# Paged sample attention reordered: page halves and head pairs outside, four requests inside

## The chip, the core and the metric

The kernel runs on one core of a Trainium2 chip. The metric is the device time of one execution in microseconds (us); lower is better. The median of three runs before the change is 5240.82 us (5238.62 to 5245.79). The profile is of one further execution. Five engines work side by side, each with its own list of instructions: TensorE (PE; its weight loads are listed apart as PEld), VectorE (DVE), ScalarE (ACT), GpSimd (POOL) and SyncE (SP). They meet at semaphores. In this part of the kernel SP and POOL start the transfers from memory.

## The reference

A decoder step of two layers runs over a prompt of 1024 tokens and, with the same weights, over eight sample requests of four new tokens each. A layer mixes three head groups and then applies a gated feed-forward network. The part that matters here is the forgetting attention of the samples: eight heads of 64, and for each request eight cached pages of 128 positions, picked by a page table from a pool.

```python
def fox_sample(q, k, v, logf, k_past, v_past, logf_past):
    c_past = jnp.cumsum(logf_past.astype(F32), axis=1)
    c_new = c_past[:, -1:, :] + jnp.cumsum(logf.astype(F32), axis=1)
    ...
    s_past = jnp.einsum('bthd,bshd->bhts', q, k_past, preferred_element_type=F32) * scale
    s_past = s_past + (cn[..., :, None] - cp[..., None, :])
    s_new = jnp.einsum('bthd,bshd->bhts', q, k, preferred_element_type=F32) * scale
    ...
    p = jax.nn.softmax(jnp.concatenate([s_past, s_new], -1), axis=-1).astype(v.dtype)
    return (jnp.einsum('bhts,bshd->bthd', p[..., :P], v_past)
            + jnp.einsum('bhts,bshd->bthd', p[..., P:], v))
```

Here `k_past = cache_fox_k[l, page_table]`, and `v_past` likewise. All is float32.

## The kernel before

Per layer the order of stages is: projections, RWKV, retention, prompt attention, **sample attention over cached pages**, output projection, feed-forward. TensorE runs them one after the other. The two layers are a hardware loop; inside it the sample attention is a loop `g` over two groups of four requests.

In a group, the 128 rows of a score tile are 4 requests x 8 heads x 4 tokens, so request `b` owns rows 32b to 32b+31 of PSUM. The queries of request `b` and head pair `p` (`cur_q[:, b, p, :]`, 128 x 32) are the stationary operand, so a product for request `b` fills the 32 columns of the array that lead to its 32 rows. Scores are summed over the four head pairs in PSUM banks 0 and 1 (512 cached positions each) and 2 (the four current tokens).

Cached keys arrive with positions on partitions and must be transposed. `key_tr(b, p)` (lines 1269 to 1275) transposes the eight pages of request `b` for head pair `p` into two PSUM banks (3 and 4 for even `p`, 5 and 6 for odd). One copy of 1024 columns brings them to `keyt[p % 2]`: ScalarE for even `p` (line 2152), VectorE for odd (line 1861). Then the products of (b, p) follow, two of 512 columns and one of 4. The loops are request outside, head pair inside, with the transposes one head pair ahead. A float32 product stands in the profile as two records, a float32 transpose as one.

After the last product VectorE takes the maximum (line 1864 on), ScalarE the exponential (line 2154), VectorE normalizes, TensorE transposes the probabilities, and they are copied out (lines 1881, 2157). The value products follow, again request by request: eight pages each, 32 rows of bank 7, 512 columns. VectorE then masks heads (line 1885) and TensorE folds the rows into the output (`F`).

Pages: `slot[b]` holds eight pages of request `b`, first keys, then values in their place. SP loads keys of a request once its last value product of the group before is done (line 508 waits, line 512 issues; for request 3 of a layer's first group it waits for the end of the prompt attention). Values of a request are loaded once its last key transposes are done: five pages by SP (lines 516 and 519), three by POOL (lines 735 to 737). A page number is read from the table in SBUF ahead of each issue. The output weights are loaded after the second group's `F`. In PE's list a helper records every product at line 760 and every transpose at line 764.

Of the kernel before, what the change touches and what calls it, by code (L numbers as in the profile page):

```python
# [21 lines left out]
T = 1024  # L22
DEPTH = 2
DB, TS = 8, 4
# [7 lines left out]
V_SP = 5  # L32
# [82 lines left out]
def build(nc, I, O, decay_rows):  # L115

    ctx = ExitStack()
    with ctx:
# [3 lines left out]
        def sem(name):  # L122
            return ctx.enter_context(nc.semaphore(name))
# [184 lines left out]
        keyt = [region((sil, NP * i), NP) for i in range(2)]  # L308
# [42 lines left out]
        page_in = [sem(f"pages_in{i}") for i in range(4)]  # L351
        vpage_in = [sem(f"last_v_pages_in{i}") for i in range(4)]
# [21 lines left out]
        def job_psum_tm(j):  # L374
# [65 lines left out]
        G_DVE = Steps("cq", "ck", "csel", "creq", *[f"kt{b}{p}" for b in range(4) for p in (1, 3)],  # L440
                      "sn", "mx", "mn", "max", "neg", "sum", "rec", "pn", "pne", "pt1", "pnt", "om", "o")
        G_ACT = Steps(*[f"kt{b}{p}" for b in range(4) for p in (0, 2)], "e", "en", "pt0")
        G_PE = Steps("bias", *[x for b in range(4) for x in [f"T{b}0"] + [y for p in range(4) for y in ([f"T{b}{p + 1}"] if p < 3 else []) + [f"S{b}{p}"]]],
                     "P0", "P1", "Pn", "V0", "V1", "V2", "V3", "F", first=5)
# [6 lines left out]
        def _(sp):  # L451
# [31 lines left out]
            with sp.Fori(0, DEPTH) as l:  # L483
# [14 lines left out]
                with sp.Fori(0, 2) as g:  # L498
                    it = l * 2 + g
                    for b in range(4):  # L500
                        if b == 3:

                            sp.wait_ge(fp_act, FP_ACT.at(l * 2 + 1, "1oT"))
                            sp.wait_ge(lft_out, l * 32 + 32)
                            sp.wait_ge(ko_out, l * 128 + 128)
                            sp.sem_inc(passed, 1)

                        sp.wait_ge(fgr_pe, G_PE.at(it - 1, f"V{b}"))
                        sp.sem_inc(passed, 1)
                        for j in range(NPG):  # L510
                            page = sp.value_load(ptab[0:1, bass.ds(g * (4 * NPG) + (b * NPG + j), 1)], min_val=0, max_val=N_POOL - 1)
                            sp.dma_start(slot[b][:, j, :], I["cache_fox_k"][bass.ds(l, 1), bass.ds(page, 1)].rearrange("a n p h d -> p (a n h d)")).then_inc(page_in[b], 16)

                    for b in range(4):
                        sp.wait_ge(fgr_pe, G_PE.at(it, f"T{b}3"))
                        sp.sem_inc(passed, 1)
                        for j in range(V_SP):
                            page = sp.value_load(ptab[0:1, bass.ds(g * (4 * NPG) + (b * NPG + j), 1)], min_val=0, max_val=N_POOL - 1)
                            sp.dma_start(slot[b][:, j, :], I["cache_fox_v"][bass.ds(l, 1), bass.ds(page, 1)].rearrange("a n p h d -> p (a n h d)")).then_inc(page_in[b], 16)
                    sp.sem_inc(passed, 1)  # L520
# [32 lines left out]
        def _(pool):  # L553
# [18 lines left out]
            with pool.Fori(0, DEPTH) as l:  # L572
# [157 lines left out]
                with pool.Fori(0, 2) as g:  # L730
                    it = l * 2 + g
                    for b in range(4):
                        pool.wait_ge(fgr_pe, G_PE.at(it, f"T{b}3"))
                        pool.sem_inc(passed, 1)
                        for j in range(V_SP, NPG):
                            page = pool.value_load(ptab[0:1, bass.ds(g * (4 * NPG) + (b * NPG + j), 1)], min_val=0, max_val=N_POOL - 1)
                            pool.dma_start(slot[b][:, j, :], I["cache_fox_v"][bass.ds(l, 1), bass.ds(page, 1)].rearrange("a n p h d -> p (a n h d)")).then_inc(vpage_in[b], 16)
# [20 lines left out]
        def _(pe):  # L758
# [68 lines left out]
            with pe.Fori(0, DEPTH) as l:  # L827
# [428 lines left out]
                with pe.Fori(0, 2) as g:  # L1256
                    it = l * 2 + g
                    G_PE.start()
                    gd = lambda n: (fgr_dve, G_DVE.at(it, n))
                    ga = lambda n: (fgr_act, G_ACT.at(it, n))  # L1260
                    ev = lambda b, p: (gd if p % 2 else ga)(f"kt{b}{p}")
# [7 lines left out]
                    def key_tr(b, p):  # L1269

                        if b or p >= 2:
                            pe.wait_ge(*(ev(b, p - 2) if p >= 2 else ev(b - 1, p + 2)))
                        for j in range(NPG):
                            last = tr(ps[:, 3 + 2 * (p % 2) + j // 4, P * (j % 4):P * (j % 4) + P], slot[b][:, j, P * p:P * p + P])
                        G_PE.mark(last, fgr_pe, f"T{b}{p}")

                    for b in range(4):
                        pe.wait_ge(page_in[b], it * ((NPG + V_SP) * 16) + NPG * 16)
                        key_tr(b, 0)
                        for p in range(4):  # L1280
                            if p < 3:
                                key_tr(b, p + 1)
                            pe.wait_ge(*ev(b, p))
                            o = slice(NS * b, NS * b + NS)
                            last_one = p == 3
                            for a in range(2):
                                mm(ps[o, a, :], cur_q[:, b, p, :], keyt[p % 2][:, 512 * a:512 * a + 512], False, last_one)
                            last = mm(ps[o, 2, 0:TS], cur_q[:, b, p, :], cur_k[:, p, TS * b:TS * b + TS], False, last_one)
                            G_PE.mark(last, fgr_pe, f"S{b}{p}")
# [12 lines left out]
                    for b in range(4):  # L1302
                        pe.wait_ge(page_in[b], it * ((NPG + V_SP) * 16) + (NPG + V_SP) * 16)
                        pe.wait_ge(vpage_in[b], it * ((NPG - V_SP) * 16) + (NPG - V_SP) * 16)
                        o = slice(NS * b, NS * b + NS)
                        for j in range(NPG):
                            last = mm(ps[o, 7, :], pts[:, j, o], slot[b][:, j, :], False, j == NPG - 1)
                        G_PE.mark(last, fgr_pe, f"V{b}")
# [52 lines left out]
        def _(v):  # L1361
            def on(*waits):
                for s, val in waits:
                    v.wait_ge(s, val)
# [55 lines left out]
            with v.Fori(0, DEPTH) as l:  # L1420
# [423 lines left out]
                with v.Fori(0, 2) as g:  # L1844
# [11 lines left out]
                    for b in range(4):  # L1856
                        for p in (1, 3):
                            on(gp(f"T{b}{p}"))
                            if b or p == 3:
                                on(gp(f"S{b}1") if p == 3 else gp(f"S{b - 1}3"))  # L1860
                            gm(v.tensor_copy(keyt[1], ps[:, 5:7, :].rearrange("p a b -> p (a b)")), f"kt{b}{p}")
                    on(gp("S33"))
# [21 lines left out]
                    on(gp("V3"))  # L1884
# [36 lines left out]
        def _(a):  # L1921
# [24 lines left out]
            with a.Fori(0, DEPTH) as l:  # L1946
# [193 lines left out]
                with a.Fori(0, 2) as g:  # L2140
# [6 lines left out]
                    for b in range(4):  # L2147
                        for p in (0, 2):
                            on(gp(f"T{b}{p}"))
                            if b or p == 2:  # L2150
                                on(gp(f"S{b}0") if p == 2 else gp(f"S{b - 1}2"))
                            gm(a.copy(keyt[0], ps[:, 3:5, :].rearrange("p a b -> p (a b)")), f"kt{b}{p}")  # L2152
# [124 lines left out]
```

## Time and profile before

| | |
|---|---|
| median of three runs | 5240.82 us |
| span of the profiled execution | 5223.1 us |
| TensorE busy | 4683.3 us, 90% |
| VectorE, ScalarE, GpSimd busy | 1092.1, 654.3, 260.1 us |
| sample attention of layer 0 in the trace | from about 1355 to 1534 us |
| sample attention of layer 1 | from about 3929 to 4108 us |

An engine table gives busy time and its share of the span. The chain of work that ended last is followed back from the last instruction to what released each step. The table of stretches gives busy time, the granted TensorE clock (1.00 is 2.4 GHz, 0.50 is 1.2 GHz) and the DMA rate. In the timeline neighbouring instructions of one kind are merged, with their count behind an x; the square bracket has the idle time ahead of them and what ended it.

### The profile page before, as it was taken

Reading aid. Unit: us, or ns where it says so; the run is one execution under the profiler, and the core shown is the slowest. Engines: PE = TensorE matmul, PEld = TensorE weight load, DVE = VectorE, ACT = ScalarE, POOL = GpSimd, SP = SyncE. Lnnn points to the kernel's source line nnn. Section 1 sums busy time; section 2 is a strip of 40 time slices with the busy share of each in tenths; the row PEclk is TensorE's granted clock in tenths of the full one; section 3 lists DMA queues with packets and bytes.
Section 4 is the critical chain, followed back from the end, with each engine's and each line's share of the span. In section 5 each row is a group of like instructions: output and inputs, shape, how many; then the busy total and the mean of one; then the engine's idle time right before and its main releaser. Section 6 shows DMA issues by size and latency. Waiting matters only on the chain.

```text
span 5223.1 us, 55407 instructions
## 1 busy us (share of the span) xinstructions
PE 4683.3 (90%) x20862; PEld 3164.5 (61%) x20862; DVE 1092.1 (21%) x2491; ACT 654.3 (13%) x1105; POOL 260.1 (5%) x456
## 2 busy tenths in 40 slices
PE   7688888988889999999995879898888999999998
PEld 4477576755445666666654766666653456666665
DVE  2344222133212000000024541312332110000001
ACT  0222011133100000000003220102231000000000
POOL 1000002100000000000010000130000000000000
PEclk8888787989899999999997888798998999999999
DMA  3300101102241111111112001011024211112011
GB/s 75 17 0 0 38 21 23 42 26 65 93 139 33 36 40 36 36 41 34 39 38 5 0 5 41 13 35 42 13 65 157 86 33 36 36 36 58 22 34 61
DMA packets 274079, 215.20 MB, mean 41 GB/s; under 512 B 23696, under 2 KB 236912, under 8 KB 272640
## 3 DMA queue, kind: packets, MB, share of 16 engines
q1 hardware_dynamic: 255296, 163.64, 12.2%
q0 software_dynamic: 18624, 49.50, 3.4%
q8 instruction: 93, 1.52, 0.1%
q14 instruction: 66, 0.54, 0.1%
HBM read 197.55 MB, written 15.53 MB: 41 GB/s over the span
## 4 chain that ended last, share of the span: by engine, by line
PE 82%; DVE 7%; issue 5%; ACT 3%; DMA 3%; DVEq 0%; POOL 0%; ACTq 0%; POOLq 0%; SPq 0%
PE ps L760 79%; PE ps L764 3%; DMA out_rwkv_shift_sample<-big 1%; DVE hT L1379 1%; ACT wd L2136 1%; DMA big<-in_x_prompt 0%; DVE big L1571 0%; DMA wd<-in_state_rwkv 0%; ACT wd L2123 0%; ACT big L2106 0%; DMA out_y_prompt<-big 0%; ACT sil L2152 0%; DVE sil L1372 0%; DVE big L1579 0%; DVE big L1541 0%
## 5 line engine op out<-in xcount | busy, mean ns | idle before, releaser
L760 PE MATMUL ps<-hT,ring 128*128 128x352 f32 x6528 | 1966.1, 463 | 25.6 <-DVE hT L1379 10.7
L760 PEld LDWEIGHTS ps<-hT,ring 128*128 128x128 f32 x6528 | 1246.7, 192 | 738.7 <-issue 29.1
L760 PE MATMUL ps<-big,wd 128*128 128x352 f32 (+3 forms) x2576 | 711.6, 439 | 65.5 <-ACT big L1969 42.3
L760 PEld LDWEIGHTS ps<-big,wd 128*128 128x128 f32 (+2 forms) x2576 | 462.5, 192 | 311.5 <-ACT big L1969 42.6
L1901 DVE TENSOR_TENSOR big<-ps,sil 128x1056 f32 x44 | 55.3, 1258 | 1189.5 <-PE ps L760 1189.5
L760 PE MATMUL ps<-wd 128*128 128x128 f32 (+4 forms) x1560 | 235.0, 297 | 70.0 <-ACT wd L2136 21.7
L760 PE MATMUL ps<-big 128*128 128x128 f32 (+4 forms) x1488 | 244.0, 337 | 52.5 <-POOL big L636 14.8
L760 PEld LDWEIGHTS ps<-wd 128*128 128x128 f32 (+2 forms) x1560 | 207.1, 203 | 136.5 <-issue 76.2
L760 PE MATMUL ps<-ring,hT 128*128 128x128 f32 (+1 forms) x2304 | 261.5, 275 | 0.0
L764 PE MATMUL ps<-ident,big 128*128 128x128 f32 (+4 forms) x998 | 175.4, 322 | 95.4 <-ACT big L1992 28.3
L760 PEld LDWEIGHTS ps<-ring,hT 128*128 128x128 f32 (+1 forms) x2304 | 256.9, 183 | 5.2 <-issue 2.4
L760 PEld LDWEIGHTS ps<-big 128*128 128x128 f32 (+2 forms) x1488 | 203.5, 222 | 86.1 <-issue 16.7
L764 PEld LDWEIGHTS ps<-ident,big 128*128 128x128 f32 (+4 forms) x998 | 131.3, 162 | 123.3 <-issue 67.5
L2164 ACT ACTIVATE sil<-ps 128x1056 f32<-128x1056 f32 x44 | 46.3, 1051 | 1162.8 <-PE ps L760 1162.8
L760 PE MATMUL ps<-sil,wd 128*128 128x64 f32 (+2 forms) x544 | 175.4, 438 | 3.6 <-ACT sil L2152 3.6
L1906 DVE TENSOR_TENSOR xT<-ps,xT 128x1056 f32<-128x1056 f32 x16 | 20.1, 1257 | 599.9 <-PE ps L760 599.9
L2123 ACT ACTIVATE wd<-wd,big 128x256 f32<-128x256 f32 (+7 forms) x128 | 99.2, 775 | 301.7 <-DVE big L1805 301.7
L764 PE MATMUL ps<-ident,wd 128*128 128x128 f32 (+1 forms) x644 | 104.2, 298 | 35.7 <-DVE wd L1877 18.1
L760 PE MATMUL ps<-big,sil 64*128 64x64 f32 (+4 forms) x560 | 116.9, 391 | 8.3 <-DVE sil L1710 8.3
L760 PE MATMUL ps<-ring,wd 128*128 128x128 f32 (+1 forms) x584 | 90.2, 300 | 36.5 <-ACT wd L2136 25.7
L760 PE MATMUL ps<-big,ring 128*128 128x352 f32 x384 | 121.4, 459 | 0.0
L760 PE MATMUL ps<-sil 64*128 64x256 f32 (+4 forms) x608 | 81.8, 420 | 40.6 <-DVE sil L1489 37.7
(336 smaller groups left out, 3122.6 us busy)
## 6 DMA issues: line engine op xcount, KB each, us to landing
big<-in_cache_fox_k SPq DMA_DIRECT2D x128, 256.0 KB, 2.9
ring<-in_w_in SPq DMA_DIRECT2D x60, 512.0 KB, 3.8
ring<-in_w_gate SPq DMA_DIRECT2D x44, 512.0 KB, 3.8
ring<-in_w_up SPq DMA_DIRECT2D x44, 512.0 KB, 3.8
wd<-in_w_down SPq DMA_DIRECT2D x16, 1408.0 KB, 7.0
big<-in_cache_fox_v SPq DMA_DIRECT2D x80, 256.0 KB, 4.0
big<-in_cache_fox_v POOLq DMA_DIRECT2D x48, 256.0 KB, 4.3
ring<-in_w_out SPq DMA_DIRECT2D x16, 512.0 KB, 4.1
```

The source lines that it names most:

```text
L760: return pe.matmul(out, lhsT, rhs, start=start, stop=stop, skip_group_check=True)
L764: return pe.transpose(out, in_, ident[0:n, 0:n])
L1379: NRM_DVE.mark(v.scalar_tensor_tensor(hT[:, k, :].rearrange("p (a b) -> p a b", a=3), xT[:, k, :].rearrange("p (a b) -> p a b", a=3), col( ...
L1901: v.tensor_tensor(big[:, bass.ds((q * 2 + u) * NT, NT)].rearrange("p (a b) -> p a b", a=3), job_psum(1), sil[:, u * NT:(u + 1) * NT].rearr ...
L1906: v.tensor_tensor(xk, job_psum(j), xk, ALU.add).then_inc(evac[j % 2], 1)
L2123: fm(act(sp_[:, s % 2, 0:w], sp_[:, s % 2, 0:w], ACT.Exp, bias=nmx[:, s:s + 1], accum_out=rsum[:, s:s + 1]), f"{u}e{s}")
L2136: fm(a.copy(ptt[:, 0, 0:s // 2 + 1, :], ps[:, 4:6, :].rearrange("p a (b c) -> p (a b) c", c=P)[:, 0:s // 2 + 1, :]), f"{u}pt{s}")
L2164: act(sil[:, u * NT:(u + 1) * NT].rearrange("p (a b) -> p a b", a=3), job_psum(0), ACT.Silu).then_inc(evac[0], 1)
```

## The change

Scores are computed by steps `s = 0..7`, `s = 4a + p`: a page half `a` (four pages, HP = 4) and a head pair `p`, with all four requests inside. A step transposes four pages of each request into one bank per request (3 to 6); four copies of 512 columns, ScalarE for requests 0 and 2, VectorE for 1 and 3, bring them to `keyt[s % 2][:, b, :]`; four products of 512 columns follow, one per request, and in the first page half the four small ones. The transposes of step s+1 are listed ahead of the products of step s. `keyt[1]` moves from `sil` to `ring`. The value products go page by page with the four requests inside, half by half. Page loads go by halves: values of half `a` after the last transposes of that half, keys of the second group's half `a` after the value products of that half. Of each half SP loads two pages per request and POOL two (POOL takes no part in the keys of the first group). The loop over the groups is written out on SP, POOL and TensorE.

```diff
-        keyt = [region((sil, NP * i), NP) for i in range(2)]
+        HP = NPG // 2
+        keyt = [region((sil, 0), 4, HP * PG), region((ringf, 0), 4, HP * PG)]
...
-                with sp.Fori(0, 2) as g:
-                    it = l * 2 + g
-                    for b in range(4):
...
-                        sp.wait_ge(fgr_pe, G_PE.at(it - 1, f"V{b}"))
...
-                    for b in range(4):
-                        sp.wait_ge(fgr_pe, G_PE.at(it, f"T{b}3"))
-                        for j in range(V_SP):
...
+                for g in range(2):
+                    if g:
+                        for a in range(2):
+                            sp.wait_ge(fgr_pe, G_PE.at(l * 2, f"V{a}"))
+                            sp.sem_inc(passed, 1)
+                            for j in (HP * a, HP * a + 1):
+                                for b in range(4):
+                                    key_page(1, b, j)
+                    for a in range(2):
+                        sp.wait_ge(fgr_pe, G_PE.at(l * 2 + g, f"T{4 * a + 3}3"))
+                        sp.sem_inc(passed, 1)
+                        for j in (HP * a, HP * a + 1):
+                            for b in range(4):
+                                value_page(g, b, j)
...
+                    for a in range(2):
+                        pool.wait_ge(fgr_pe, G_PE.at(l * 2 + g, f"T{4 * a + 3}3"))
+                        for j in (HP * a + 2, HP * a + 3):
+                            for b in range(4):
...
-                with pe.Fori(0, 2) as g:
+                for g in range(2):
...
-                    for b in range(4):
-                        pe.wait_ge(page_in[b], it * ((NPG + V_SP) * 16) + NPG * 16)
-                        key_tr(b, 0)
-                        for p in range(4):
-                            if p < 3:
-                                key_tr(b, p + 1)
-                            pe.wait_ge(*ev(b, p))
-                            o = slice(NS * b, NS * b + NS)
-                            last_one = p == 3
-                            for a in range(2):
-                                mm(ps[o, a, :], cur_q[:, b, p, :], keyt[p % 2][:, 512 * a:512 * a + 512], False, last_one)
+                    def key_tr(s):
+                        a, p = s // 4, s % 4
+                        if p == 0:
+                            pe.wait_ge(kpage_in[a], l * (6 * HP * 16) + g * (2 * HP * 16) + 4 * HP * 16)
+                            if g:
+                                pe.wait_ge(kpage_more[a], l * (2 * HP * 16) + 2 * HP * 16)
+                        for b in range(4):
+                            if s:
+                                pe.wait_ge(*ev(s - 1, b))
+                            for j in range(HP):
+                                last = tr(ps[:, 3 + b, P * j:P * j + P], slot[b][:, HP * a + j, P * p:P * p + P])
+                            G_PE.mark(last, fgr_pe, f"T{s}{b}")
+                    def key_scores(s):
+                        a, p = s // 4, s % 4
+                        pe.wait_ge(*ev(s, 2))
+                        pe.wait_ge(*ev(s, 3))
+                        for b in range(4):
+                            last = mm(ps[o4[b], a, :], cur_q[:, b, p, :], keyt[s % 2][:, b, :], False, p == 3)
+                        if a == 0:
+                            for b in range(4):
+                                last = mm(ps[o4[b], 2, 0:TS], cur_q[:, b, p, :], cur_k[:, p, TS * b:TS * b + TS], False, p == 3)
+                        G_PE.mark(last, fgr_pe, f"S{s}")
+                    for s in KS:
+                        key_tr(s)
+                        if s:
+                            key_scores(s - 1)
+                    key_scores(7)
...
-                    for b in range(4):
...
-                        for j in range(NPG):
-                            last = mm(ps[o, 7, :], pts[:, j, o], slot[b][:, j, :], False, j == NPG - 1)
+                    for a in range(2):
+                        pe.wait_ge(vpage_in[a], it * (2 * HP * 16) + 2 * HP * 16)
+                        pe.wait_ge(vpage_more[a], it * (2 * HP * 16) + 2 * HP * 16)
+                        for j in range(HP * a, HP * a + HP):
+                            for b in range(4):
+                                last = mm(ps[o4[b], 7, :], pts[:, j, o4[b]], slot[b][:, j, :], False, j == NPG - 1)
+                        G_PE.mark(last, fgr_pe, f"V{a}")
...
+                    for s in KS:
+                        for b in (1, 3):
+                            on(gp(f"T{s}{b}"))
+                            if s >= 2:
+                                on(gp(f"S{s - 2}"))
+                            gm(v.tensor_copy(keyt[s % 2][:, b, :], ps[:, 3 + b, :]), f"kt{s}{b}")
...
+                    for s in KS:
+                        for b in (0, 2):
+                            on(gp(f"T{s}{b}"))
+                            if s >= 2:
+                                on(gp(f"S{s - 2}"))
+                            gm(a.copy(keyt[s % 2][:, b, :], ps[:, 3 + b, :]), f"kt{s}{b}")
```

## Rows read from the trace of the kernel before

**Rows 1.** Page: busy us, share and instructions of engines; chain by engine.

```profile
PE 4683.3 (90%) x20862; PEld 3164.5 (61%) x20862; DVE 1092.1 (21%) x2491; ACT 654.3 (13%) x1105; POOL 260.1 (5%) x456
...
PE 82%; DVE 7%; issue 5%; ACT 3%; DMA 3%; DVEq 0%; POOL 0%; ACTq 0%; POOLq 0%; SPq 0%
```

**Rows 2.** Stretches, layer 0: length, busy PE, PEld, DVE, ACT, POOL, clock, DMA share, GB/s.

```profile
1359.00:1364.80 5.80, 5.80 (x20) 3.90 (x21) 1.22 (x1) 1.01 (x1) 0.00 (x0) 0.50 0.00 0
...
1373.00:1408.40 35.40, 34.46 (x171) 17.14 (x169) 7.35 (x6) 6.08 (x6) 5.25 (x10) 1.00 0.55 184
...
1417.90:1422.80 4.90, 4.90 (x7) 1.06 (x7) 0.00 (x0) 0.00 (x0) 0.00 (x0) 0.50 0.00 0
```

**Rows 3.** Timeline of TensorE, score stretch: start, us, engine, line, operation, count.

```profile
1359.12 3.67 PE L764 MATMUL ps<-ident,big 128*128 128x128 f32 x16
...
1366.62 1.90 PE L760 MATMUL ps<-sil,wd 128*32 128x512 f32 x4
...
1368.49 0.86 PEld L764 LDWEIGHTS ps<-ident,big 128*128 128x128 f32 x8
...
1369.51 1.90 PE L760 MATMUL ps<-sil,wd 128*32 128x512 f32 x4
```

**Rows 4.** Timeline of TensorE, value products of group 0, near a request change.

```profile
1417.90 25.01 PE L760 MATMUL ps<-big,hT 128*32 128x512 f32 x64
...
1425.49 0.14 PEld L760 LDWEIGHTS ps<-big,hT 128*32 128x32 f32 x3 [0.32 <-issue]
1425.92 0.14 PEld L760 LDWEIGHTS ps<-big,hT 128*32 128x32 f32 x2 [0.29 <-issue]
1426.35 0.14 PEld L760 LDWEIGHTS ps<-big,hT 128*32 128x32 f32 x2 [0.29 <-issue]
```

**Rows 5.** Timeline of TensorE, norm sums in three column groups of 32, output projection.

```profile
1568.97 0.79 PE L760 MATMUL ps<-sil,ones 128*32 128x352 f32 x6
1569.69 2.63 PE L760 MATMUL ps<-hT,ring 128*128 128x352 f32 x8
```

**Rows 6.** Timeline, where the stages of both groups begin and end.

```profile
1408.40 0.16 DVE L1864 TENSOR_TENSOR hT<-ps,wd 128x4 f32<-128x4 f32 x1 [2.34 <-PE ps L760]
...
1442.95 0.69 DVE L1885 TENSOR_TENSOR wd<-ps,wd 128x512 f32<-128x512 f32 x1 [27.17 <-PE ps L760]
...
1449.58 3.67 PE L764 MATMUL ps<-ident,big 128*128 128x128 f32 x16
...
1498.02 0.16 DVE L1864 TENSOR_TENSOR hT<-ps,wd 128x4 f32<-128x4 f32 x1 [2.34 <-PE ps L760]
...
1507.52 24.58 PE L760 MATMUL ps<-big,hT 128*32 128x512 f32 x64
...
1532.13 0.69 DVE L1885 TENSOR_TENSOR wd<-ps,wd 128x512 f32<-128x512 f32 x1 [26.74 <-PE ps L760]
```

**Rows 7.** Timeline, copies of 512 PSUM columns on ScalarE and VectorE.

```profile
1414.05 0.59 ACT L2157 COPY hT<-ps 128x512 f32<-128x512 f32 x1 [2.38 <-PE ps L764]
...
1414.90 0.69 DVE L1881 COPY hT<-ps 128x512 f32<-128x512 f32 x1 [1.83 <-PE ps L764]
```

**Rows 8.** Timeline of page issues by SP, POOL; page: KB, us to landing.

```profile
1370.45 5.05 SPq L519 DMA_DIRECT2D big<-in_cache_fox_v  x5
...
1385.43 0.54 POOL L737 DMA_DIRECT2D big<-in_cache_fox_v  x1 [0.79 <-issue]
...
big<-in_cache_fox_v POOLq DMA_DIRECT2D x48, 256.0 KB, 4.3
```

**Rows 9.** Stretches as in rows 2: keys by SP alone, both queues.

```profile
1346.00:1356.00 10.00, 2.70 (x9) 1.74 (x10) 5.06 (x11) 0.00 (x0) 0.00 (x0) 0.50 0.71 215
...
1475.00:1480.00 5.00, 4.70 (x29) 2.79 (x28) 1.23 (x1) 1.18 (x2) 0.54 (x1) 1.00 1.00 355
```

**Rows 10.** Stretches as in rows 2, near the end: transposes alone, with pauses.

```profile
5193.00:5201.40 8.40, 4.82 (x39) 3.58 (x34) 2.90 (x5) 3.17 (x4) 1.60 (x3) 1.00 0.32 127
5201.50:5213.00 11.50, 8.34 (x36) 6.54 (x35) 2.38 (x4) 4.84 (x5) 2.13 (x4) 0.50 0.52 208
```

More of the change, by code:

```diff
@@ L31 @@
 N_POOL = DB * NPG * 5 // 4
-V_SP = 5
 EPS = 1e-6
@@ L350, in build @@
         decay_out, past_in = sem("decay_rows_out"), sem("past_gates_in")
-        page_in = [sem(f"pages_in{i}") for i in range(4)]
-        vpage_in = [sem(f"last_v_pages_in{i}") for i in range(4)]
+        kpage_in = [sem(f"k_pages_in{i}") for i in range(2)]
+        vpage_in = [sem(f"v_pages_in{i}") for i in range(2)]
+        kpage_more = [sem(f"k_pages_in_pool{i}") for i in range(2)]
+        vpage_more = [sem(f"v_pages_in_pool{i}") for i in range(2)]
         table_in, lft_out = sem("table_in"), sem("log_gates_out")
@@ L439, in build @@
         FS_DVE = Steps("qz", *[f"q{p}{k}" for p in range(4) for k in range(2)], "lfs", "lfn", "ncs")
-        G_DVE = Steps("cq", "ck", "csel", "creq", *[f"kt{b}{p}" for b in range(4) for p in (1, 3)],
+        KS = range(8)
+        G_DVE = Steps("cq", "ck", "csel", "creq", *[f"kt{s}{b}" for s in KS for b in (1, 3)],
                       "sn", "mx", "mn", "max", "neg", "sum", "rec", "pn", "pne", "pt1", "pnt", "om", "o")
-        G_ACT = Steps(*[f"kt{b}{p}" for b in range(4) for p in (0, 2)], "e", "en", "pt0")
-        G_PE = Steps("bias", *[x for b in range(4) for x in [f"T{b}0"] + [y for p in range(4) for y in ([f"T{b}{p + 1}"] if p < 3 else []) + [f"S{b}{p}"]]],
-                     "P0", "P1", "Pn", "V0", "V1", "V2", "V3", "F", first=5)
+        G_ACT = Steps(*[f"kt{s}{b}" for s in KS for b in (0, 2)], "e", "en", "pt0")
+        G_PE = Steps("bias", *[x for s in KS for x in [f"T{s}{b}" for b in range(4)] + ([f"S{s - 1}"] if s else [])], "S7",
+                     "P0", "P1", "Pn", "V0", "V1", "F", first=5)
         block = ctx.enter_context(nc.Block())
@@ L1255, in _ @@
                 last.then_inc(fs_pe, 1)
-                with pe.Fori(0, 2) as g:
+                for g in range(2):
                     it = l * 2 + g
@@ new lines, in _ @@
+                    o4 = [slice(NS * b, NS * b + NS) for b in range(4)]
+                    def key_tr(s):
+                        a, p = s // 4, s % 4
+                        if p == 0:
+                            pe.wait_ge(kpage_in[a], l * (6 * HP * 16) + g * (2 * HP * 16) + 4 * HP * 16)
+                            if g:
+                                pe.wait_ge(kpage_more[a], l * (2 * HP * 16) + 2 * HP * 16)
[5 more added lines that the diff above has]
+                            G_PE.mark(last, fgr_pe, f"T{s}{b}")
@@ new lines, in key_scores @@
+                    def key_scores(s):
[5 more added lines that the diff above has]
+                        if a == 0:
+                            for b in range(4):
+                                last = mm(ps[o4[b], 2, 0:TS], cur_q[:, b, p, :], cur_k[:, p, TS * b:TS * b + TS], False, p == 3)
+                        G_PE.mark(last, fgr_pe, f"S{s}")
@@ L1301, in _ @@
                     mm(ps[:, 7, :], pnt[0:NS, :], vn[0:NS, :], True, False)
[L1302 to L1306, printed above, removed]
-                            last = mm(ps[o, 7, :], pts[:, j, o], slot[b][:, j, :], False, j == NPG - 1)
-                        G_PE.mark(last, fgr_pe, f"V{b}")
+                    for a in range(2):
+                        pe.wait_ge(vpage_in[a], it * (2 * HP * 16) + 2 * HP * 16)
+                        pe.wait_ge(vpage_more[a], it * (2 * HP * 16) + 2 * HP * 16)
+                        for j in range(HP * a, HP * a + HP):
+                            for b in range(4):
+                                last = mm(ps[o4[b], 7, :], pts[:, j, o4[b]], slot[b][:, j, :], False, j == NPG - 1)
+                        G_PE.mark(last, fgr_pe, f"V{a}")
                     pe.wait_ge(*gd("om"))
@@ L1855, in _ @@
                     gm(v.tensor_copy(cur_req, sreq[:, bass.ds(g, 1), :].rearrange("p a b -> p (a b)")), "creq")
[L1856 to L1862, printed above, removed]
+                    for s in KS:
[4 more added lines that the diff above has]
+                            gm(v.tensor_copy(keyt[s % 2][:, b, :], ps[:, 3 + b, :]), f"kt{s}{b}")
+                    on(gp("S7"))
                     past = ps[:, 0:2, :].rearrange("p a b -> p (a b)")
```

53 lines of the change are left out of this document (21 added, 32 removed).

## Prediction

> **What bounds the kernel now.** First the engine table and the chain of work that ended last: TensorE is busy for 90% of the span and carries 82% of the chain, DMA 3% [rows 1]. A change pays if it shortens what TensorE does or waits for. Next the busy time by stretch over the stage that is edited, the cached-page attention of layer 0. In the score stretch (1373.0 to 1408.4) TensorE is busy for 34.5 of 35.4 us at the full granted clock, VectorE for 7.4, ScalarE for 6.1 [rows 2]. TensorE is the bound there too, and pages come in time. The clock is 0.50 (1.2 GHz) for the first 5.8 us of that stage and for the first 4.9 us of the value products, each after a wait [rows 2].
>
> Then the timeline, for what TensorE does with its time. One round of a request and head pair starts with four half-products (a float32 product is recorded as two) of 32 x 512 at 1366.62; eight transposes follow at 1368.49; the next round's products start at 1369.51 [rows 3]. So a round takes 2.89 us: 1.87 for products (four at 0.43, 0.15 for the small current-token ones and the switch), 1.02 for transposes (0.86 for eight weight loads, the rest switch). Each product has 32 stationary columns, a quarter of the array's width, and in this order all products of one request go to the same quarter, so they queue. The value products are 64 such records, one request after the other: 25.01 us [rows 4].
>
> What happens when two requests meet: within a request a weight load starts every 0.43 us; at the change of request, near 1425.5, 3, 2 and 2 start in three successive 0.43 us [rows 4]. The last records of one request and the first of the next run side by side, at undiminished pace. And where three column groups are addressed in turn, in the norm sums, six records of 352 columns are through in 0.72 us (1568.97 to the next work at 1569.69) [rows 5]; at 0.30 us each, from the weights products' pace scaled by width (0.43 x 352 / 512), six in a line would be 1.78. Three quarters thus run together.
>
> **The change part by part.** The order of requests and head pairs is turned inside out. Four requests now stand inside, each in its own quarter.
>
> Scores: 16 rounds per group of four requests become 8, of a head pair and a page half. A new round has 16 transposes (1.02 + 0.86 = 1.88) and 8 half-products of 512 columns in four quarters, two slots deep: 2 x 0.43 + 0.15 = 1.01. That is 2.89 us, the price of an old round, for twice the work. Eight are 23.1. The clock's low start stays: 5.7 us of it at half speed cost 2.85 more, so 26.1. Before: 1408.40 - 1359.12 = 49.3 in the first group, 1498.02 - 1449.58 = 48.4 in the second [rows 3, 6]. Saved 23.2 and 22.3. Old rounds also lost about 1 us per request at its start; that goes with them.
>
> Evacuation: 32 copies of 1024 columns become 64 of 512 over both groups of a layer and both engines. A round has two on ScalarE (0.59 each) and two on VectorE (0.69) [rows 7], 1.4 us at most, beside 2.89 us of TensorE. The transposes of round s+1 into a bank wait for its copy of round s, which has the 1.01 us of products as its cover; the last copy, some 0.2 after its transposes plus 0.69, just fits. I cost it at nothing; without the cover it is 0.7 per round, 22 us in all, an upper bound. The added waits at the head of each product group hold back only those products and the transposes behind them, on TensorE, by the same amount.
>
> Values: 64 records in four quarters are 16 slots, 6.9 us, plus 2.45 for 4.9 us of low clock and 0.13 of lead: 9.5. Before: 1442.95 - 1417.90 = 25.05 and 1532.13 - 1507.52 = 24.6 [rows 4, 6]. Saved 15.5 and 15.1.
>
> The unknown is whether four quarters of 512 columns run as freely as two of 512 and three of 352 do. Bounds: all four free, or pairs only (priced below); I take four, since the row of three is nearest and shows no loss beyond 0.13 us a burst. The Trainium skill, "TensorE: Matmul & The Clock Gate", Part 3 on packing small matmuls, measured 2.38 times for three column tiles; the burst here makes 1.78 / 0.72 = 2.5. Carried to a continuous stream as 0.79 of the ideal, its figure would put 1.8 us on the values and 1.8 on the scores of each group, so some 14 in all, near 5113; the undiminished pace at the change of request [rows 4] speaks for the larger gain.
>
> Loads: a page is 256 KB, a half of four requests 16 pages or 4.19 MB, eight by SP and eight by POOL. SP issues one per 1.18 us ((5.05 - 0.35) / 4), POOL one per 0.54 + 0.79 = 1.33, and POOL's land 4.3 later [rows 8]. With 1 us from release to first issue POOL's eighth lands after 1 + 7 x 1.33 + 4.3 = 14.6. Together the queues ask for over 400 GB/s; the most that a 5 us stretch here moved is 355 [rows 9], by which a half needs 11.8 us plus start and landing. I take 15. Upper bound: the 215 GB/s that SP alone reached [rows 9], 19.5 plus 4.5, so 24.
>
> Where that lies: (a) first-group keys are all issued before the stage, nothing changes. (b) Value half 0 is released in the middle of the scores, 23 us ahead of its use. (c) Value half 1 is released by the last transposes; from there to its use are 2.1 of products, 9.7 of softmax as before and about 5.9 of value half 0: 17.7 against 15, hidden with 2.7 to spare. (d) Second-group keys, half 0, are released when value half 0 is consumed; TensorE then has 3.4 of value half 1 and the 6.6 between 1442.95 and 1449.58 [rows 6], so 10.1, and waits 4.9 for the rest. Before, pages of the first request went out a quarter into the value products and this cost nothing; it is the one new wait. Behind it on TensorE stands the whole second group. (e) Its half 1 queues behind half 0 and lands about 26 to 28 after the release, needed at 15 + 4 x 2.89 + 2 = 28.6: just hidden. On SP nothing but the output weights stands behind, and those wait for the group's end in either kernel; POOL has only later outputs.
>
> Sum for a layer: 23.2 + 15.5 + 22.3 + 15.1 - 4.9 = 71.2, for both 142.4. The profiled span of 5223.1 becomes 5080.7. The runs' median lies 17.7 above that span, so **5098 us**, 2.7% less. This kernel's runs can tell about 0.2% from no change; that is my bound of "same".
>
> **The rivals.**
> Pairs only: two quarters at a time, as the change of request shows for 512 columns [rows 4]. Rounds of 3.75 and values of 16.3: per layer 16.4 + 8.7 + 14.0 + 8.3 = 47.4, time 5146. Against: three in [rows 5].
> Loads become the bound: two queues add no bandwidth, a half takes 24. Then (d) waits 13.9, (e) about 6, (c) 15 and 11: 41 more per layer, time 5180; at 280 GB/s only 13 more in all, 5111. For: a whole half is asked for at once. Against: 355 GB/s with both queues at work [rows 9].
> The clock: in the new rounds TensorE spends more time on transposes (1.72) than on products (0.86). If the clock were 1.2 GHz throughout the scores, a round would be 5.8 and a stage 46: 20 more per stage, 5179. For 8.4 us near the end transposes alone, with pauses, ran at granted 1.00 [rows 10], though at 0.50 after that. The same page of the Trainium skill, Part 4 on transposes, says that they do not count as busy for the clock in the same way, which is this rival; the stretches of [rows 10] bear it out only in the second one.
> Slower: the quarters take turns, because the array changes quarter with each record. Place: scores and values. Eight slots in a round make 5.5 us, a stage 47, saving 2 at best; the values lose the overlap that they have now at three changes of request: 27.5 + 2.6 = 30.1, 5 more. Net some 3 per group, 5253 us, and more if each change of quarter exposed its weight load. It decides once the overlap is under 1.05-fold. [rows 5] is against it.
> Better than forecast: keys arrive in time and the small products vanish under the others: 12 less, 5086.
>
> **How the numbers follow.** Forecast 0.67, loads 0.11 (mostly at the mild end), pairs 0.08, better 0.06, clock 0.04, slower 0.04. The range 5078 to 5152 takes in forecast, better, pairs and mild loads. Faster 0.94, within 0.2% 0.02, slower 0.04.
>
> **What would show it.** In the profile after: the 64 value records of a group in about 9.5 us, four weight loads per 0.43; eight rounds of 2.9; first transposes of the second group waiting about 5 us for cached keys; no wait for pages before value half 1. It is wrong if records of different quarters start 0.43 apart, if clock 0.50 lies in the rounds, or if DMA ends waits elsewhere.

## The result, and the profile after

The changed kernel takes 5091.14 us in the median (5090.70 to 5091.69), the kernel before, run beside it on the same chip, 5241.09. The ratio is 0.9722 with a 95% interval from 0.9703 to 0.9742: 2.8% faster. 5098 was forecast.

The timeline of TensorE in the first group's scores of layer 0, with VectorE's first step of the softmax at its end. It answers to rows 3 and 6.

```profile
1362.75 6.20 PE L783 MATMUL ps<-ident,big 128*128 128x128 f32 x32
1368.88 1.06 PE L779 MATMUL ps<-sil,wd 128*32 128x512 f32 x8
...
1369.91 1.97 PE L783 MATMUL ps<-ident,big 128*128 128x128 f32 x16
1371.81 1.07 PE L779 MATMUL ps<-ring,wd 128*32 128x512 f32 x8
...
1380.60 1.07 PE L779 MATMUL ps<-sil,wd 128*32 128x512 f32 x8
1381.59 1.97 PE L783 MATMUL ps<-ident,big 128*128 128x128 f32 x16
1383.49 1.06 PE L779 MATMUL ps<-ring,wd 128*32 128x512 f32 x8
...
1388.38 0.16 DVE L1895 TENSOR_TENSOR hT<-ps,wd 128x4 f32<-128x4 f32 x1 [1.19 <-PE ps L779]
```

Eight half-products of 512 columns, four quarters two deep, are through in 1.03 us with the small ones (1368.88 to 1369.91), where four in one quarter took 1.87 with theirs [rows 3]. A round is 2.93 us with the small products (1368.88 to 1371.81) and 2.89 without (1380.60 to 1383.49). No row between them shows idle time: the copies are hidden. The scores last from 1362.75 to 1388.38, 25.6 us, where they took 49.3 [rows 3, 6].

The value products of that group: TensorE's row, its weight loads, and VectorE's head mask that ends them.

```profile
1397.87 9.11 PE L779 MATMUL ps<-big,hT 128*32 128x512 f32 x64
...
1401.29 0.20 PEld L779 LDWEIGHTS ps<-big,hT 128*32 128x32 f32 x4 [0.66 <-issue]
1402.09 0.12 PEld L779 LDWEIGHTS ps<-big,hT 128*32 128x32 f32 x4 [0.60 <-issue]
1402.52 0.12 PEld L779 LDWEIGHTS ps<-big,hT 128*32 128x32 f32 x4 [0.31 <-issue]
...
1407.06 0.69 DVE L1916 TENSOR_TENSOR wd<-ps,wd 128x512 f32<-128x512 f32 x1 [11.31 <-PE ps L779]
```

Four weight loads start per 0.43 us, where there was one (and 3, 2, 2 at a change of request) [rows 4]: all four quarters stream at once, none slowed by the others. 9.2 us from 1397.87 to 1407.06, against 25.05.

What is new is a wait. The start of the second group on TensorE, the DMA row of the page for the keys that POOL now loads (KB, us to landing), and the stretch of the wait with the columns of rows 2:

```profile
1410.26 2.10 PE L779 MATMUL ps<-wd 64*128 64x512 f32 x6 [1.39 <-DVE wd L1886]
1419.82 4.99 PE L783 MATMUL ps<-ident,big 128*128 128x128 f32 x32 [7.46 <-DMA big<-in_cache_fox_k]
...
big<-in_cache_fox_k POOLq DMA_DIRECT2D x32, 256.0 KB, 5.7
...
1407.10:1419.80 12.70, 3.16 (x14) 2.03 (x15) 1.61 (x6) 0.00 (x0) 5.37 (x10) 0.70 1.01 353
```

TensorE stands idle for 7.46 us until cached keys are there, while the DMA engines are busy throughout at 353 GB/s, about the 355 of [rows 9] and for more than twice as long.

The stage of a layer is measured below from the start of VectorE's last small copy ahead of the first group (line 1855 before, 1886 after) to the start of the head mask of the second. "Rest" is the profiled span without both stages. Medians are of each kernel's own runs.

| kernel | stage, layer 0 | layer 1 | rest | median |
|---|---|---|---|---|
| before, first profile | 177.2 | 177.0 | 4868.9 | 5241.1 |
| before, profiled again | 176.1 | 174.2 | 4882.7 | 5226.8 |
| changed kernel | 104.1 | 106.2 | 4879.9 | 5091.1 |
| changed kernel, again | 104.2 | 104.3 | 4882.2 | 5098.4 |
| values by request | 117.8 | 119.0 | 4888.8 | 5118.2 |
| scores in one quarter | 144.6 | 144.8 | 4877.8 | 5173.6 |
| loads on SP alone | 140.6 | 140.2 | 4874.1 | 5160.1 |
| before with values interleaved | 151.3 | 151.4 | 4877.0 | 5199.1 |
| keys released by page | 100.5 | 100.4 | 4886.1 | 5088.5 |
| no second keys | 97.3 | 97.0 | 4876.6 | 5072.4 |
| by page, idle-time products | 100.1 | 99.0 | 4879.9 | 5080.8 |

The stage repeats within 3 us; the rest, which no kernel edits, varies by 20 over these eleven executions and by 14 between the two of the kernel before. So mechanisms are read from the stage, and medians confirm what is larger than about 10 us.

### The profile page after: what moved, and what is told of

It is laid out like the page before. It is cut to its first block, busy times and chain, and to the rows that moved or that the text cites. A ratio compares the mean times of both kernels' runs of the same rounds, so it can differ in the third digit from the quotient of the medians.

```text
span 5090.1 us, 55376 instructions
## 1 busy us (share of the span) xinstructions
PE 4538.9 (89%) x20862; PEld 3131.7 (62%) x20862; DVE 1097.4 (22%) x2523; ACT 659.4 (13%) x1137; POOL 287.2 (6%) x504
## 4 chain that ended last, share of the span: by engine, by line
PE 81%; DVE 7%; issue 5%; DMA 3%; ACT 3%; DVEq 0%; POOL 0%; POOLq 0%; SPq 0%; ACTq 0%
PE ps L779 77%; PE ps L783 4%; DMA out_rwkv_shift_sample<-big 1%; DVE hT L1410 1%; ACT wd L2167 1%; DMA big<-in_x_prompt 0%; DVE big L1602 0%; DMA wd<-in_state_rwkv 0%; ACT big L2137 0%; ACT wd L2154 0%; DVE sil L1403 0%; DVE big L1610 0%; DMA out_y_prompt<-big 0%; DMA big<-in_cache_fox_k 0%; DVE big L1574 0%
## 5 line engine op out<-in xcount | busy, mean ns | idle before, releaser
L783 PE MATMUL ps<-ident,big 128*128 128x128 f32 (+4 forms) x998 | 171.9, 322 | 109.7 <-ACT big L2023 26.8
L783 PEld LDWEIGHTS ps<-ident,big 128*128 128x128 f32 (+4 forms) x998 | 133.5, 164 | 144.6 <-issue 66.2
L779 PE MATMUL ps<-ring,wd 128*128 128x128 f32 (+1 forms) x712 | 107.1, 354 | 36.5 <-ACT wd L2167 25.7
L783 PE MATMUL ps<-ident,wd 128*128 128x128 f32 (+1 forms) x644 | 104.3, 298 | 36.1 <-DVE wd L1908 18.2
L783 PEld LDWEIGHTS ps<-ident,wd 128*128 128x128 f32 (+1 forms) x644 | 83.4, 158 | 42.7 <-DVE wd L1908 21.9
```

Source lines behind the costliest of these rows:

```text
L779: return pe.matmul(out, lhsT, rhs, start=start, stop=stop, skip_group_check=True)
```

## Experiments

**The kernel before, profiled again.** No edit. Question: why did its first profile lie 18 us under the median?

> The kernel before, unchanged, run and profiled once more. Its profiled span of 5223.1 us stands 18 us under the median of its runs (5241), the changed kernel's span (5090.1) only 1.0 us under its median (5091.1). Theory: the edited stage gained 73.1 and 70.6 us in the two layers by the traces, 143.7 in all, and the 6 us more in the medians (150) come from stages that were not edited, whose low-clock stretches fall differently from execution to execution. Then a second profile of it shows a span near 5239, the sample stage of a layer again near 177 us (from its bias products to its head mask), and the extra time outside. Rival: the extra time lies in the sample stage (over 180 us a layer), and the change removed more than the traces say.

Measured: median 5226.76 of ten runs (5216.94 to 5244.26); its profiled run took 5234.54 with this span:

```profile
core 0: 5233.0 us, clock 0.917
```

A run is its span plus 1.5 us. The stage took 176.1 and 174.2, 1 to 3 less than in the first profile, and the rest 13.8 more. The theory holds: the extra time lies outside the edited stage. The expected cause is in the two traces: outside both stages the granted clock stood at 0.50 for 777.1 us in the first profile and for 803.4 us in this one. The 26.3 us more can cost half of their length, 13.2, and the rest grew by 13.8. Why the low-clock stretches fall differently is not shown.

**Is it the order of the value products?** They go request by request again within a half.

```diff
-                        for j in range(HP * a, HP * a + HP):
-                            for b in range(4):
+                        for b in range(4):
+                            for j in range(HP * a, HP * a + HP):
                                 last = mm(ps[o4[b], 7, :], pts[:, j, o4[b]], ...
```

> The changed kernel, but the value products of a page half again request by request (four pages each) instead of page by page with the four requests inside. Theory (products of different column quarters run side by side, so order alone makes the gain): the value products of a group go from 9.2 to about 24 us, since only the changes of request overlap. The keys of the second group then have time to land, so its wait of 7.5 us for them goes. Net per layer 2 x 15 - 7 = 23, time 5137. Rival (the value products became short because of the loads by halves and fewer waits, not by the order): they stay near 9 to 12 us and the time within 10 us of 5091.

Measured: 5118.15 us. The products take 17.6 to 18.0 us per group, neither 24 nor 9, and the wait for the second group's keys shrinks to 1.6 us in layer 0 instead of going. The timeline of weight loads of this kernel shows why:

```profile
1414.27 0.14 PEld L779 LDWEIGHTS ps<-big,hT 128*32 128x32 f32 x3 [0.32 <-issue]
1414.69 0.14 PEld L779 LDWEIGHTS ps<-big,hT 128*32 128x32 f32 x2 [0.29 <-issue]
1415.12 0.14 PEld L779 LDWEIGHTS ps<-big,hT 128*32 128x32 f32 x2 [0.29 <-issue]
1415.58 0.11 PEld L779 LDWEIGHTS ps<-big,hT 128*32 128x32 f32 x1 [0.32 <-issue]
1416.01 0.14 PEld L779 LDWEIGHTS ps<-big,hT 128*32 128x32 f32 x3 [0.32 <-issue]
```

The pattern 3, 2, 2 of a change of request [rows 4] now returns with every request. At each change the next request runs beside the last four records of the one before it. Count them: before, 64 records with three changes need 64 - 12 = 52 slots of 0.43 us, 22.4, plus 2.45 for the low clock: 24.8 (measured 25.05 and 24.6). Here seven changes leave 36 slots, 15.5 + 2.45 = 17.9 (17.6 to 18.0). The order is the cause, as the theory says; its size was wrong because I left the changes that a half adds out of the expectation.

**Do the score products overlap too?** All four requests address quarter 0; scores of three requests are left out.

```diff
-                            last = mm(ps[o4[b], a, :], cur_q[:, b, p, :], ...
+                            last = mm(ps[o4[0], a, :], cur_q[:, b, p, :], ...
```

> The changed kernel, but the score products of all four requests are sent to the column quarter of request 0 (the cached scores of the other three are left out of their rows). Same number of products, copies, transposes and loads. Theory (quarters run side by side): eight half-products in a line cost 8 x 0.43 instead of 2 x 0.43, so a round goes from 2.9 to 5.5 us, 2.6 x 8 x 4 = 83 more, of which later needs for pages take back some waiting; time 5165 to 5175. Rival (the rounds became short by halving the switches between transposes and products): the round stays near 3 us, time 5091 to 5100.

Measured: 5173.56 us. TensorE's timeline of two rounds:

```profile
1376.73 3.19 PE L779 MATMUL ps<-ring,wd 128*32 128x512 f32 x7
...
1380.32 1.97 PE L783 MATMUL ps<-ident,big 128*128 128x128 f32 x16
1382.22 3.19 PE L779 MATMUL ps<-sil,wd 128*32 128x512 f32 x7
```

A round is 5.49 us (1376.73 to 1382.22), scores take 46.1 and 44.9 instead of 25.6 and 24.4. Transposes, copies, switches and loads are the same in number, so the short round of the changed kernel comes from the overlap of quarters.

**What are two queues worth?** POOL loads nothing; SP loads all pages of a half.

```diff
-                            for j in (HP * a, HP * a + 1):
+                            for j in range(HP * a, HP * a + HP):
                                 for b in range(4):
                                     key_page(1, b, j)
...
-                        for j in (HP * a, HP * a + 1):
+                        for j in range(HP * a, HP * a + HP):
                             for b in range(4):
                                 value_page(g, b, j)
...
```

> The changed kernel with all page loads on SP, none on POOL. It tells what the sharing by two queues is worth. Theory (a half is bound by the issue of its pages: 16 x 1.15 on one queue, then landing): a half lands about 24 us after its release instead of 16.4. Then the second group's keys cost TensorE 15 us instead of 7.5, the second half of them about 5, and the second halves of the values 15 and 10: 35 to 38 more a layer, time 5160 to 5170. Rival (the DMA engines' rate of 360 to 390 GB/s sets the landing either way): under 10 more in all, 5091 to 5100.

Measured: 5160.07 us, 36.5 and 34.0 a layer in the stage. TensorE's waits in layer 0, each from its timeline row:

```profile
1413.22 5.07 PE L763 MATMUL ps<-big,hT 128*32 128x512 f32 x32 [12.66 <-DMA big<-in_cache_fox_v]
1432.23 5.84 PE L767 MATMUL ps<-ident,big 128*128 128x128 f32 x32 [8.03 <-DMA big<-in_cache_fox_k]
1452.14 3.67 PE L767 MATMUL ps<-ident,big 128*128 128x128 f32 x16 [7.17 <-DMA big<-in_cache_fox_k]
1490.12 5.87 PE L763 MATMUL ps<-big,hT 128*32 128x512 f32 x32 [7.71 <-DMA big<-in_cache_fox_v]
```

The time came as expected, its parts did not, so the agreement is partly luck. The first keys cost 8.0, not 15: TensorE came to them late, because it had stood 12.7 us before value half 1, which SP was still loading (it issues the keys only from 1411.47 on). The second keys cost 7.2, not 5, and the values 12.7 and 7.7, not 15 and 10. The four waits are 35.6 us against 7.7 in the changed kernel, 28 more of the 36.5; the other 8.6 are work at the low clock, most of it behind the waits, such as the 16 transposes of 3.67 us, which take 1.97 in the changed kernel. One queue's issue is the bound here: SP issues 32 pages in 37.86 us without a pause, 1.2 us a page. Without POOL's share nearly half of the change's gain would have gone into waits for pages and the low clock behind them.

**The values' part alone, on the kernel before.**

```diff
-                        o = slice(NS * b, NS * b + NS)
-                        for j in range(NPG):
+                    for j in range(NPG):
+                        for b in range(4):
+                            o = slice(NS * b, NS * b + NS)
                             last = mm(ps[o, 7, :], pts[:, j, o], slot[b][:, j, :], False, j == NPG - 1)
-                        G_PE.mark(last, fgr_pe, f"V{b}")
+                            if j == NPG - 1:
+                                G_PE.mark(last, fgr_pe, f"V{b}")
```

> The kernel before with one part of the change alone: value products page by page with the four requests inside; scores, page order and queues as before (all of a slot's pages are released at the end of the value products). Theory: the value products of a group go from 24.8 to about 9.3 us, 15.5 x 4 = 62 less. The price is the second group's keys: SP issues the first request's eight pages only after the last value product, 1 + 7 x 1.2 + 4 = 13.5 us against the 6.6 that TensorE needs to get there, 7 us a layer; later requests' pages (10 us per request from SP) keep pace with 11.7 us of work. Net 5241 - 62 + 14 = 5193. Rival (without loads by halves and two queues the gain is eaten by waits for pages): 5220 or more.

Measured: 5199.06 us, ratio 0.9939 to the kernel before (0.9917 to 0.9962). Both mechanisms are in its timeline:

```profile
1417.63 8.60 PE L760 MATMUL ps<-big,hT 128*32 128x512 f32 x64
...
1439.45 3.68 PE L764 MATMUL ps<-ident,big 128*128 128x128 f32 x16 [7.24 <-DMA big<-in_cache_fox_k]
```

The values of the group are through in 8.8 us, and the wait for keys is 7.2, as expected. The stage is 26 us a layer shorter than in the first profile and 23 to 25 than in the second, 51 and 48 in all against the expected 48. The medians of the two kernels run side by side differ by only 31. Its profiled run took 5181.32 at a mean granted clock of 0.915, the other three 5197.76 to 5201.07 at 0.911 to 0.912. A mean lower by 0.0035 stands for some 18 us (0.0035 x 5190) lost to the low clock, an estimate that fits their 16 to 20; as they have no trace, where they lost it is not known.

**The price of the new wait.** Three kernels beside the changed one, on one chip.

> The changed kernel, unchanged, beside the next three on one chip. All theories: 5091 within 3 us, wait of TensorE for the second group's keys near 7.5 us a layer.

Measured: 5098.35 us (5085.02 to 5103.86), 7 above the 5091 that was expected within 3; wait for the keys 7.0 and 7.4 us in the two layers. The kernel before took 5230.83 beside it. The three kernels that follow are compared with this run.

First, keys released page by page, two requests' pages by each queue:

```diff
-                        for a in range(2):
-                            sp.wait_ge(fgr_pe, G_PE.at(l * 2, f"V{a}"))
+                        for j in range(NPG):
+                            sp.wait_ge(fgr_pe, G_PE.at(l * 2, f"V{j}"))
                             sp.sem_inc(passed, 1)
-                            for j in (HP * a, HP * a + 1):
-                                for b in range(4):
-                                    key_page(1, b, j)
+                            for b in (0, 1):
+                                key_page(1, b, j)
...
```

> The changed kernel, but keys of the second group are released page by page (after the value products of that page in all four requests) instead of by halves, two requests' pages by SP and two by POOL each. Theory (the wait for these keys is the time from release to landing, and both queues start early): the first release comes about 3.5 us sooner, so the wait of 7.5 falls to about 3.5 to 4, 8 us less over both layers: 5083. Rival (the rate of the DMA engines sets the landing, with the second half's pages competing): the wait falls by under 1.5, time 5088 to 5091.

Measured: 5088.54 us; the wait is 3.59:

```profile
1423.64 5.26 PE L781 MATMUL ps<-ident,big 128*128 128x128 f32 x32 [3.59 <-DMA big<-in_cache_fox_k]
```

The stage is 3.7 to 3.9 us a layer shorter than that of the changed kernel run beside it, as the theory has it: an earlier release moves the landing by as much, in spite of the busy DMA engines. The time by itself would not tell, for 5088.54 lies in the band of the rival; the wait, 3.4 us shorter, and the stage do.

Second, the second group's key loads, on SP and POOL, and TensorE's waits for them are left out:

```diff
-                    if g:
-                        for a in range(2):
-                            sp.wait_ge(fgr_pe, G_PE.at(l * 2, f"V{a}"))
-                            ...
```

> The changed kernel without the key loads of the second group and the waits for them (its scores are computed from what the slots hold, so keys of the second group are left out). It prices the new wait by itself. Theory: 7.5 us a layer go, and nothing else is late in their place, 15 less, 5076; the low clock at the start of that group's scores stays. Rival (another wait takes its place, the first-group values or copies): under 8 less, 5083 or more.

Measured: 5072.39 us. The second group's transposes follow its bias products at once:

```profile
1409.18 2.10 PE L764 MATMUL ps<-wd 64*128 64x512 f32 x6 [1.39 <-DVE wd L1870]
1411.21 5.38 PE L768 MATMUL ps<-ident,big 128*128 128x128 f32 x32
```

The stage is 6.9 and 7.3 us shorter, where the waits were 7.0 and 7.4. So the wait is worth what it measures, and nothing takes its place. Of the 26 us between the medians that is 14; the other 12 are no more than the rest varies by.

Third, release by page and, in addition, products that nobody reads, in TensorE's idle time:

```diff
+                    if g:
+                        for _ in range(3):
+                            mm(ps[:, 6, :], ident[:, :], keyt[0][:, 0, :])
...
                     key_scores(7)
+                    for _ in range(5):
+                        mm(ps[:, 6, :], ident[:, :], keyt[0][:, 0, :])
```

> The kernel with release by page, and in addition idle-time products on TensorE whose result nobody reads: five (4.3 us) after the last scores of each group, while the softmax runs, and three (2.6 us) ahead of the second group's transposes, while its keys load. It prices the low clock at the starts. Theory: the granted clock is at 1.00 when the value products start, so they take 6.9 to 7.2 instead of 9.1 us, 8 us over four groups, and the second group's first transposes gain 1 to 2 us a layer: 5083 - 10 = 5073. Rival (the clock falls all the same, or the products delay the transposes of the probabilities): no gain over the release by page, 5083 or more.

Measured: 5080.76 us, the shortest median of the kernels that compute everything, 18 under the changed one run beside it; by the stage only 4.1 and 5.3 a layer, 9.4 in all, and the other 8 are no more than the rest varies by. Its ratio to the kernel before is 0.9724 (0.9703 to 0.9746), against 0.9748 (0.9726 to 0.9770) for the changed kernel beside it: overlapping, so by times alone the two are not told apart. Compared with release by page alone it is shorter by 0.4 and 1.4 a layer, not by the 5 expected. The timeline of both groups' values:

```profile
1395.47 3.64 PE L777 MATMUL ps<-big,hT 128*32 128x512 f32 x32
1401.35 5.34 PE L777 MATMUL ps<-big,hT 128*32 128x512 f32 x32 [2.24 <-DMA big<-in_cache_fox_v]
...
1447.15 3.64 PE L777 MATMUL ps<-big,hT 128*32 128x512 f32 x32
1454.41 3.64 PE L777 MATMUL ps<-big,hT 128*32 128x512 f32 x32 [3.62 <-DMA big<-in_cache_fox_v]
```

The five products do what they should: value half 0 takes 3.64 us, at 2.4 GHz from its first record. TensorE then arrives earlier at value half 1, which has not landed, and waits; in the first group the clock falls again behind that wait (0.68 over the 5.34 us of half 1). The low clock at the start of the values had been cover for that load. The three products ahead of the second group's transposes cost as well as gain: they end at 1416.39, and by the trace the last of the keys that these transposes need had landed at 1413.68, so they hold the transposes up by 2.7 us, while the transposes take 3.66 us instead of the 5.26 of release by page.

## Why the prediction was right, step by step

**Overlap of quarters.** It carries the gain. Forecast: a new round for the price of an old one, 2.89; measured 2.93 and 2.89. Scores 26.1 against 25.6, 24.4, 25.6 and 26.0; values 9.5 against 9.2, 9.0, 9.2 and 9.4. The unknown, four quarters of 512 columns against the three of 352 in [rows 5], came out at the free end of its bounds. The remark that old rounds lost about 1 us per request does not hold: in the trace of before a request takes 11.71 us from its first transposes to those of the next (1384.88 to 1396.59), 0.15 more than four rounds of 2.89. It was no term of the sum. "Pairs only" falls by the four loads per 0.43 us; "slower" falls with it, and the kernel with all scores in one quarter shows what it would have looked like. The Trainium skill's 2.38 for three column tiles ("TensorE: Matmul & The Clock Gate", Part 3) carried over as 0.79 of the ideal gave 5113; this trace shows no such loss in a continuous stream (four loads per 0.43 us above).

**Copies and waits in the rounds.** Costed at nothing: right, rounds follow each other without idle time.

**The clock.** It was 1.00 in the rounds and from 1402.0 to 1407.1 in the values, and low at the starts as before. The last two lines lie in the first transposes of the second group:

```profile
1370.00:1382.00 12.00, 12.00 (x124) 8.64 (x125) 5.53 (x8) 4.69 (x8) 2.48 (x5) 1.00 0.42 133
...
1397.90:1402.00 4.10, 4.10 (x21) 0.96 (x24) 0.00 (x0) 0.00 (x0) 0.00 (x0) 0.50 0.78 297
1402.00:1407.10 5.10, 4.98 (x48) 1.20 (x40) 0.04 (x1) 0.00 (x0) 1.07 (x2) 1.00 0.24 71
...
1419.80:1422.00 2.20, 2.19 (x11) 2.20 (x12) 0.21 (x1) 0.59 (x1) 0.82 (x2) 0.50 1.06 393
1422.50:1424.70 2.20, 2.20 (x21) 2.06 (x19) 1.38 (x2) 1.47 (x3) 1.02 (x2) 1.00 1.05 388
```

The rounds hold 1.72 us of transposes to 0.86 of products and ran at 1.00 all the same: the clock rival is out. More than that, behind the 7.46 us wait the clock rises from 0.50 to 1.00 while TensorE does nothing but transposes (from 1419.82 on, for 4.99 us). The same page of the Trainium skill, Part 4, says that transposes do not count as busy for the clock in the same way; this trace does not agree.

**Second-group keys, step (d).** The term that was mis-sized most: forecast 4.9, measured 7.5 and 7.6. Value half 0 ends near 1403.4; the keys land and the transposes start at 1419.82, 16.4 later, not 15: POOL's pages land 5.7 us after their issue instead of the 4.3 of [rows 8], with the DMA engines busy throughout. And TensorE is there after 9.0 us instead of 10.1, because the bias products run in 2.10 us, the clock still being high. The rival "loads" is this at its mild end. Half 1 of these keys, step (e), cost no wait, as forecast: it had landed at 1430.24, 26.8 us after the release of half 0, and its transposes came at 1434.56.

**Value half 1, step (c).** Forecast hidden with 2.7 to spare. Hidden in the changed kernel, but with less to spare: by the trace it had landed at 1401.89 in the first group of layer 0, 1.5 us ahead of its use, and in the second it cost 0.2 us of waiting. With the starts at full clock it is not: the spare time was no more than what the low clock costs (some 2 us for 4.1 us at 0.50).

**The sum.** Forecast 71.2 a layer, by the traces 177.2 - 104.1 = 73.1 and 177.0 - 106.2 = 70.8; 143.9 in all against 142.4. A little less time in scores and values than forecast pays for the longer wait. The medians differ by 150 us in the first pair of runs and by 132 in the second (5230.83 and 5098.35); the stages account for 140 to 146 whichever two traces are compared, and what is missing or left over is no more than the rest varies by.

**From span to median.** This step was wrong. I added the 17.7 us between the profiled span and the median of before as if they belonged to every run. They do not: a run is 1.5 us longer than its span, and the others came from an execution of before whose unedited stages were 14 us shorter than in its second profile, with 26 us less of them at the low clock. The changed kernel's span is 5090.1, not the forecast 5080.7: its rest is 11 us longer than that of the first trace, and its stages gave 1.5 us more than forecast. So the first error put the forecast of the median 17 us too high and the second 9 too low. That they cancel down to 7 is luck.

## What to carry to other kernels

Where small products are 32 columns wide, put consecutive ones into different column groups: here, at no cost in instructions, four of them took the time of one. Then look at the loads behind them, for the stage that has become shorter has the same bytes to move: here nearly half of the gain hung on two queues issuing the pages, and while the second group's keys load the DMA engines are already busy throughout. And read a profiled execution against another of the same kernel before a difference between span and median goes into a sum.

## What the runs showed of the hardware

- Four column groups with different moving data, 512 float32 columns each, stream at the pace of one: four weight loads per 0.43 us, 64 records in 9.1 us including 4 us at 1.2 GHz.
- TensorE starts products of another column group ahead of up to four earlier records that still queue for their own group: 3, 2, 2 loads at each change of request, four slots saved by each, as both orders of the value products show (24.8 and 17.9 us by that count, 24.6 to 25.05 and 17.6 to 18.0 measured).
- Two queues loading 256 KB pages kept 353 GB/s for 12.7 us; the time to landing rose from 4.3 to 5.7 us on POOL under that load.
- Behind an idle time of 7.46 us the clock rose from 0.50 to 1.00 while TensorE ran nothing but transposes (0.50 from 1419.8 to 1422.0, 1.00 from 1422.5 to 1424.7).
- The unedited part of the kernel took 4868.9 and 4882.7 us in two executions of the same program. The second had 26.3 us more of it at the low clock, which is worth up to 13.2 of the 13.8 us. Over the eleven profiles it varies by 20 us, 0.4%. Why the low-clock stretches fall differently stays open.
